# Gates and branch projections with the weights stationary and all 256 tokens moving

## What is computed

```python
h = _rmsnorm(x, norm_g)
u = h @ w_in
# a_x, a_z, b_q, b_k, b_v, b_z, c_q, c_k, c_v, c_z, gate_logits = split(u)
ya = _pool_mixer(a_x, pool_w, pool_scale) * silu(a_z)
yb = _swa_attention(b_q, b_k, b_v, sinks) * silu(b_z)
yc = _moba_attention(c_q, c_k, c_v) * silu(c_z)
ga, gb, gc = split(sigmoid(gate_logits), 3)          # 3 x 1024 wide
merged = ga * (ya @ w_proj_a) + gb * (yb @ w_proj_b) + gc * (yc @ w_proj_c)
x = x + merged @ w_out
```

## Time and profile before

| | |
|---|---|
| median of 3 runs | 783.0 us (782.73 to 786.51) |
| the profiled execution's own time | 789.08 us |
| its span | 787.1 us, mean granted clock 0.964 |
| TensorE busy | 735.1 us (93%) |
| VectorE, ScalarE, GpSimd busy | 365.4, 307.5, 258.8 us |
| chain that ended last | TensorE 83%, VectorE 7%, issue 3%, ScalarE 3%, GpSimd 2% |
| waits of TensorE for the transposes' input (L887) | 6.8 us in 2 |

### The profile page before, as it was taken

The page is one execution under the profiler, slowest core; times in us unless marked ns, Lnnn a source line. Parts: engine busy times, 40 slices in busy tenths (PEclk is TensorE's granted clock), DMA queues, the critical chain, the costliest instruction groups (busy, mean ns, idle before and its releaser), DMA issues.

```text
span 787.1 us, 10525 instructions
## 1 busy us (share of the span) xinstructions
PE 735.1 (93%) x4158; PEld 513.7 (65%) x4158; DVE 365.4 (46%) x656; ACT 307.5 (39%) x535; POOL 258.8 (33%) x103
## 2 busy tenths in 40 slices
PE   4999997799999899899999998899999999999994
PEld 3799996577676686588887776667444534444441
DVE  5223724445746947422655467554343234134225
ACT  5543345064848246343456776321011101111122
POOL 0756645234648544466264357400000000000000
PEclk9999999799999989999999999895999999999997
DMA  9954667156535428556422433369999999999931
GB/s 359 414 206 184 251 258 275 46 201 227 211 119 228 191 107 310 224 214 255 170 112 108 172 148 135 121 249 431 422 427 419 430 381 430 422 427 430 386 146 54
DMA packets 19576, 202.70 MB, mean 258 GB/s; under 512 B 2385, under 2 KB 3153, under 8 KB 7505
## 3 DMA queue, kind: packets, MB, share of 16 engines
q1 hardware_dynamic: 18816, 200.47, 64.3%
q10 hardware_dynamic: 720, 1.70, 0.6%
HBM read 201.11 MB, written 1.05 MB: 257 GB/s over the span
## 4 chain that ended last, share of the span: by engine, by line
PE 83%; DVE 7%; issue 3%; ACT 3%; POOL 2%; DMA 1%; ACTq 0%; DVEq 0%
PE psum L779 15%; PE psum L780 14%; PE psum L781 14%; PE psum L1087 14%; PE psum L1119 7%; PE psum L1060 5%; POOL ring_rounded L1401 2%; PE psum L1039 2%; PE psum L872 2%; DVE ring_rounded L1601 1%; PE psum L998 1%; PE psum L980 1%; PE psum L960 1%; ACT ring_rounded L1303 1%; DMA sig<-in_norm_rows 1%
## 5 line engine op out<-in xcount | busy, mean ns | idle before, releaser
L1401 POOL TENSOR_TENSOR ring_rounded<-ring,ring_rounded 128x1024 fp32r<-128x1024 f32 (+1 forms) x99 | 258.6, 2635 | 249.9 <-ACT ring_rounded L1303 249.8
L1303 ACT ACTIVATE ring_rounded<-ring 128x1024 fp32r<-128x1024 f32 (+1 forms) x136 | 133.3, 1035 | 20.5 <-PE psum L781 19.5
L1601 DVE TENSOR_TENSOR ring_rounded<-ring,ring_rounded 128x1024 fp32r<-128x1024 f32 (+1 forms) x37 | 82.8, 2241 | 65.3 <-ACT ring_rounded L1303 65.2
L779 PE MATMUL psum<-hT_rounded,ring_rounded 128*128 128x256 f32 x360 | 103.8, 288 | 3.7 <-POOL ring_rounded L1401 3.7
L781 PE MATMUL psum<-hT_rounded,ring_rounded 128*128 128x256 f32 x360 | 102.5, 285 | 0.0
L780 PE MATMUL psum<-work_rounded,ring_rounded 128*128 128x256 f32 x360 | 102.5, 285 | 0.0
L779 PE MATMUL psum<-ring_rounded,hT_rounded 128*128 128x512 f32 (+1 forms) x224 | 90.5, 404 | 1.4 <-DVE work_rounded L1506 1.4
L780 PE MATMUL psum<-ring_rounded,hT_rounded 128*128 128x512 f32 (+1 forms) x224 | 87.2, 389 | 0.0
L781 PE MATMUL psum<-ring_rounded,work_rounded 128*128 128x512 f32 (+1 forms) x224 | 86.8, 387 | 0.0
L1087 PE MATMUL psum<-ring,work 128*64 128x512 f32 x320 | 84.7, 594 | 0.0
L779 PEld LDWEIGHTS psum<-hT_rounded,ring_rounded 128*128 128x128 f32 x360 | 69.7, 194 | 8.2 <-POOL ring_rounded L1401 4.5
(11 more groups left out here) (248 smaller groups left out, 1099.9 us busy)
## 6 DMA issues: line engine op xcount, KB each, us to landing
ring<-in_chunks SPq DMA_DIRECT2D x44, 2048.0 KB, 8.2
ring<-in_expert_w_down SPq DMA_DIRECT2D x16, 2048.0 KB, 13.9
ring<-in_expert_w_gate SPq DMA_DIRECT2D x12, 2048.0 KB, 14.6
ring<-in_expert_w_up SPq DMA_DIRECT2D x8, 2048.0 KB, 17.0
gates<-in_expert_w_up SPq DMA_DIRECT2D x4, 2048.0 KB, 25.0
hT<-in_expert_w_gate SPq DMA_DIRECT2D x4, 1024.0 KB, 16.3
mixed<-in_expert_w_gate SPq DMA_DIRECT2D x4, 1024.0 KB, 18.4
ring<-in_chunks SPq DMA_DIRECT2D x4, 512.0 KB, 8.7
```

The costliest lines, as they stand in the source:

```text
L779: nc.tensor.matmul(out, a[0], b[0], start=start, stop=False, skip_group_check=True)
L1303: nc.scalar.activation(as_rounded(high(c)[:, piece]), src[:, piece], ACT.Copy).then_inc(chunk_hi, 1)
L1401: nc.gpsimd.tensor_tensor(as_rounded(w[:, piece]), w[:, piece], was_rounded(high(c)[:, piece]), ALU.subtract)\
L1601: v.tensor_tensor(as_rounded(w[:, piece]), w[:, piece], was_rounded(high(c)[:, piece]), ALU.subtract)\
```

## The change

The gates' units become feature-major ("fm"), 48 products' matmuls of 256 columns in place of 24 of 512 columns; ScalarE evicts them to the same places in `gates`, now as tiles of features. A projection unit becomes two feature tiles with the weights stationary and the branch's 256 tokens moving: 24 matmuls of 256 columns in place of 12 of 512. merged then lies with features on the partitions, and the "mT" units go, with their 32 transposes. In their place two steps stand for each quarter of merged: `merged_high` (ScalarE rounds the quarter, SBUF to SBUF) and `merged_low` (VectorE subtracts, SBUF to SBUF). The output product waits for the quarters one by one (k 0, 2, 4, 6).

```diff
@@ plan
-    seq += [(("tm", f"g{i}", t), 2 if (i, t) in ((2, 0), (3, 0), (0, 0)) else 1) for i in (4, 5, 2, 3, 0, 1) for t in range(TT)]
+    seq += [(("fm", f"g{i}", t), 2 if (i, t) in ((2, 0), (3, 0), (0, 0)) else 1) for i in (4, 5, 2, 3, 0, 1) for t in range(TT)]
@@ merge_and_out
-        unit("proj", br, 0, 0)
-        unit("proj", br, 0, 1)
-        unit("proj", br, 1, 0)
-        unit("mT", blk, 0, 0)
-        unit("mT", blk, 0, 1)
-        unit("proj", br, 1, 1)
+        for part in range(4):
+            unit("proj", br, part // 2, part % 2)
+            if part:
+                steps.append(("merged_low", blk, part - 1))
+            steps.append(("merged_high", blk, part))
+        steps.append(("merged_low", blk, 3))
         unit("wout", blk, 0, 0)
-        unit("mT", blk, 1, 0)
-        unit("mT", blk, 1, 1)
         steps.append(("norm_half", 2 * blk - 1, 0))
         unit("wout", blk, 0, 1)
@@ tensor
                 elif kind == "proj":
-                    _, br, t, half = u
+                    _, br, a, b2 = u
                     w = parts(("proj", br), D)
                     pe.wait_ge(y_split_done, Y_SPLITS.index(br) + 1)
-                    for k in range(4):
-                        wait_piece(n, ("proj", br), k)
-                        y = [as_rounded(x[:, k, t * P:(t + 1) * P]) for x in (y_high[br], y_low[br])]
-                        last = product(b, y, w(k, half * W512, W512), k == 0, k == 3)
-                elif kind == "mT":
-                    _, blk, t, half = u
-                    pe.wait_ge(*evicted(("proj", "a" if blk == 1 else "s", t, half)))
-                    for k in range(4):
-                        f = (4 * half + k) * P
-                        last = nc.tensor.transpose(b[:, k * P:(k + 1) * P], gate_tm[:, 0, t, f:f + P], ident)
+                    for j in range(2):
+                        at = (4 * a + 2 * b2 + j) * P
+                        for k in range(4):
+                            if j == 0:
+                                wait_piece(n, ("proj", br), k)
+                            last = product(b[:, j * T:(j + 1) * T], w(k, at, P),
+                                           [as_rounded(x[:, k, :]) for x in (y_high[br], y_low[br])], k == 0, k == 3)
                 elif kind == "wout":
                     _, blk, t, half = u
                     w = parts(("wout", blk, half), W512)
-                    pe.wait_ge(*evicted(("mT", blk, t, 1)))
                     for k in range(KD):
+                        if k % 2 == 0:
+                            pe.wait_ge(merged_split, 4 * (blk - 1) + k // 2 + 1)
@@ scalar
+            def merged_high(blk, part):
+
+                act_e.wait_ge(*evicted(("proj", "a" if blk == 1 else "s", part // 2, part % 2)))
+                nc.scalar.activation(as_rounded(two_blocks(merged_hi, part)), two_blocks(gates, part), ACT.Copy).then_inc(merged_hi_ready, 1)
@@ vector
-                elif kind == "mT":
-                    _, blk, t, half = u
-                    last = v.tensor_tensor(as_rounded(merged_lo(blk, half)[:, :, t * P:(t + 1) * P]),
-                                           b.rearrange("p (k t) -> p k t", k=4),
-                                           was_rounded(merged_hi[:, 4 * half:4 * half + 4, t * P:(t + 1) * P]),
-                                           ALU.subtract)
                 elif kind == "proj":
-                    _, br, t, half = u
+                    br, part = u[1], 2 * u[2] + u[3]
                     place = dict(c=2, b=1, a=0, f=0, s=1)
-                    at = lambda br: gate_tm[:, place[br], t, half * W512:(half + 1) * W512]
+                    at = lambda br: two_blocks(gates, 4 * place[br] + part)
+            def merged_low(blk, part):
+
+                dve.wait_ge(merged_hi_ready, 4 * (blk - 1) + part + 1)
+                v.tensor_tensor(as_rounded(low_of(blk, part)), two_blocks(gates, part), was_rounded(two_blocks(merged_hi, part)), ALU.subtract)\
+                 .then_inc(merged_split, 1)
```

41 lines of the change are left out of this document (21 added, 20 removed), and 4 rows, old and new, of the table seq.

## The result

| | median of the runs | lowest to highest | profiled execution: span, own time |
|---|---|---|---|
| before (16 runs) | 786.63 us | 782.52 to 789.16 | 787.1, 789.08 |
| after (16 runs) | 789.93 us | 787.92 to 790.76 | 786.1, 787.92 |

After over before is 1.0053, 95% interval 1.0035 to 1.0071: slower by 0.5%, some 4 us by the ratio and 3.3 us by the medians. The forecast was 3.0 us more. The absolute time lies above the 786.0 us given, because two of the three times that it stood on were low ones: over 16 runs the kernel before has a median of 786.6 us.

The account below looks back on a forecast made before the run. TensorE was taken to bound the kernel, with 83% of the chain of waits. Gate form +5.2, projection form +1.2, wait at c +1.1, merges -1.1 and -3.4 gave +3.0 on 783.0: 786.0 us, range 779 to 791.5.

Parts of the forecast that it names:

- The form in the gate units: 20 gate units with 48 matmuls of 256 columns: +0.29 us per whole unit, +0.10 per half, 5.2 us in all.
- The form in b and f: Projections b and f with 24 matmuls of 256 columns for 12 of 512: +0.10 us a unit, +0.4 us each.
- Projection c: TensorE's wait for GpSimd's last weight piece grows from 0.99 to some 2.0 us; stretch +1.5 us with the form.
- rival B: Clock falls to half behind projection c's longer wait, some 6.6 us long: +6.3 us, up to 791.7 us; chance 0.15.
- the point lies between: Idle time that brings TensorE's clock to 0.50 lies between 1.45 us (harmless) and 2.83 us (followed by the fall).
- Merge 1: First merge, 262 to 297 us: second output unit evicted at 290.9 instead of 292.03, gain 1.1 us.
- The walk: Step-by-step timing of the merges in before's times, with VectorE's SBUF-only work held by GpSimd's pieces.
- Merge 2: Second merge, 480 to 515 us: second output unit evicted at 509.3 against 512.61, gain 3.4 us.
- Rival A: In the merges VectorE slips between GpSimd's pieces, three turns of 2.4 us go: -4.2 us, 778.8 us; chance 0.17.
- The sum: Whole kernel: +5.2 +1.2 +1.1 -1.1 -3.4 = +3.0 us.
- The base: Median of the runs shown, 783.0 us, to which the forecast difference of 3.0 us was added, giving 786.0 us.

Follow-up runs that it names:

- the form alone: Kernel before with only its 20 gate units in the new form (48 matmuls of 256 columns), values in wrong places: 788.62 us, 1.0038 to before.
- two-move kernel: Changed kernel with projection c's last weight piece one unit earlier and each first output chunk's four pieces ahead of part 0's rounding: 783.00 us, 0.9961 to before.
- before with the early piece: Kernel before with the last piece of projection c's weights split one unit earlier: 783.14 us, 0.9972 to before.
- all moves: Changed kernel with projection c's last piece earlier, first output chunk's pieces first, adds reading PSUM, second output chunk's pieces started earlier: 787.06 us, 1.0021 to before.
- output pieces first: Changed kernel with ScalarE rounding all four pieces of each first output chunk before the first rounding of merged: 785.02 us, 0.9999 to before.
- add from PSUM: Changed kernel with VectorE's multiply by the gate left in PSUM (branches b, a, s) and the add reading it there: 788.02 us, 1.0024 to before.

## Why the prediction was right, and where it was not

- **The form in the gate units.** Forecast 5.2 us, measured 5.3 in the changed kernel (3.6 + 1.7) and 4.6 with the form alone. In block 1 the half-clock period that begins in the wait of 9.3 us in front of the gates reaches 4.6 us into the stretch in after's trace (143.3 to 147.9) and 2.9 in before's, which is 0.9 us of the 3.6. Without it the changed kernel lies at 4.4, by the form alone at 4.6 us, some 0.7 below the forecast. A whole unit of 48 products, from its first to the next work, takes 5.92 us where I had 5.95:

```profile
423.27 0.36 PE L781 MATMUL psum<-hT_rounded,ring_rounded 128*128 128x256 f32 x1
...
429.19 0.65 PE L998 MATMUL psum<-attn,work 128*64 128x256 f32 x4
```

  That is 123 ns a product. The formula for a single gap in the Trainium skill (TensorE: Matmul & The Clock Gate, Back-to-back issue gap) gives, as an estimate, 109 ns for a product of 256 columns and 216 ns for one of 512, so some 1.2 us as the form's price in 20 units; in the kernel with the form alone the gate stretches grow by 4.6 us.
- **The form in b and f.** Forecast 0.4 each, measured 0.6 and 0.4.
- **Projection c.** The wait was forecast at 2.0 us and came out at 2.00. What the forecast left to rival B came true too: the clock fell behind it, for 3.4 us and not the 6.6 of B, and cost 1.7 us. The step that failed is B's "the point lies between": waits of 0.99 and 1.45 us were known to be harmless, 2.83 harmful, and the middle was given the chance of the milder side. All five traces with the 2.0 us wait have the fall at this place, none of the seven without it.
- **Merge 1.** Forecast -1.1, measured -2.0. The walk itself held: S + 6.9 for the chunk's third piece (as walked), S + 13.6 for the first output product (14.0), S + 28.3 for the second eviction (29.2). What it had too long: VectorE was through with part 0's subtraction 0.5 us and with part 3's eviction 0.8 us sooner, so ScalarE's start of the last pieces came at S + 17.3 where I had S + 18.1, and GpSimd took 8.10 us for its three where I had 2.4 x 3 + 1.1 = 8.3.
- **Merge 2.** Forecast -3.4, measured -4.0. VectorE was ahead of the walk by 0.3 us at part 0's eviction and by 1.0 us at the last subtraction, and 0.7 us of it were left at the end. Two adds (2.54 and 2.15 us) and part 0's subtraction (2.90 us) were held.
- **Rival A** (VectorE slips between the pieces) did not come in the changed kernel: two adds and the subtraction of part 0 were held in merge 2, the split and the subtraction in merge 1. It came, by one turn, when the pieces were rounded first (merge 1, -2.1 us).
- **The sum** was right to 0.2 us because two errors cancel, which is luck: +1.5 at projection c, -1.5 in the two merges. A forecast of 3.0 us that is made of such terms deserved the wide range that it had.
- **The base.** A difference put on a median of three runs, two of them low, gave 786.0 us for a kernel that takes 789.9. The forecast of the difference held; that of the level leaned on three runs out of a spread of 6.6 us. The loss was called too small to tell from no change (0.5%); over 16 runs of each kernel it is clear, 0.35 to 0.71%.

What stays open: what the clock does behind merge 2. The stretches of the two-move kernel add up to 1.3 us under before, its time lies 1.4 to 4.8 us under it; for before with the early piece it is 1.2 us against 0.4 to 4.1 us. The half-clock periods between merge 2 and 555 us last between 3.4 and 17.1 us in the traces, and the time behind merge 2 goes with them: 270.7 to 270.8 us with 3.4 us, 273.5 and 273.6 with 13.6, 274.5 with 17.1. What sets them I don't know; executions of one and the same kernel differ in them.

## What to carry to other kernels

A layout change that removes transposes pays twice the matmul count for the same columns: take the price per unit from neighbouring units of both forms, then look at whatever waits already, because the new form may ask for the same operand earlier and so turn a harmless wait into one that brings the clock down. Where two engines share turns, ask which instruction meets a piece after the move; a turn taken off one instruction is passed to the next one with two SBUF inputs unless that engine's work leaves the stretch. Compare kernels by stretches that the change touches, with the same small fix given to both, before one is called better; and read the granted clock of the stretches between, which can add or take some us that the change has no part in.

## What the hardware showed that I had not expected

- The granted clock fell after idle times of 2.00 us (for 3.4 us), 2.83 and 4.01 us (for 3.4 or 6.8 us). It did not fall after 1.91, 1.80 or 1.65 us in the merges, nor in merge 2 of the kernel with all moves, after one of 2.35 us. Outside the merges a wait of 3.0 us near 320 us is followed by 3.4 to 6.9 us at half clock in eleven traces and by none in output pieces first (3.03 us), and a wait of 1.35 us near 349 us by 3.4 us at half clock in add from PSUM and by none in the other eleven. So the length of one idle time alone doesn't decide it. At the fall products stand 0.21 us apart in place of 0.12.
- A VectorE instruction with two SBUF inputs takes the rest of GpSimd's instruction whatever its own size: 128x8 elements 2.37 us beside a piece, 0.17 without; 128x512 2.85 and 0.69. One with an input in PSUM takes 0.69 us in both. That agrees with the Trainium skill (SBUF — State Buffer, Who interferes with whom), which names two SBUF inputs against GpSimd's reads as the case that blocks.
- The same engine pays for it: GpSimd's pieces, 2.4 us each alone, take 8.10 us for three with VectorE's split (2.58 us, 1.2 alone) between them, near the 3 x 2.4 + 1.2 = 8.4 us of the four one behind the other: they take turns.
